# Writing out every engine loop of a two-layer mixer and expert-retrieval step

## The reference, cut to what matters

```python
def peer_ffn(h, w_q, sub_keys, u_tab, v_tab):
    q = (tok @ w_q).reshape(T, PEER_HEADS, 2, PEER_KEY_DIM // 2)
    s = jnp.einsum('thsk,snk->thsn', q, sub_keys)
    sv, si = lax.top_k(s, PEER_TOPK)                    # 16 best of 128 keys, on two sides
    cand_s = sv[..., 0, :, None] + sv[..., 1, None, :]  # 256 pairs, and again the 16 best
    cand_i = si[..., 0, :, None] * N_KEYS + si[..., 1, None, :]
    top_s, top_pos = lax.top_k(cand_s, PEER_TOPK)
    idx = jnp.take_along_axis(cand_i, top_pos, axis=-1)
    g = jax.nn.softmax(top_s, axis=-1)
    a = jax.nn.gelu(jnp.einsum('tkd,td->tk', u_tab[idx], tok))
    return jnp.einsum('tk,tkd->td', g * a, v_tab[idx])
```

## Time and profile before

| | |
|---|---|
| median of three runs | 6189.84 us |
| the three runs | 6198.78, 6189.19, 6189.84 us |
| span of the profiled execution, first to last instruction | 6172.5 us |
| median over that span | 17.3 us |
| expert stage, layer 1, first gather to the end of the last | 1083 to 3060 us |
| expert stage, layer 2 | 4143 to 6125 us |
| busy: PE, DVE, POOL, ACT | 4637.5, 2873.5, 2863.0, 450.7 us |
| mean granted TensorE clock | 0.938 |
| bytes moved by gathers | 1342.34 MB of 1489.50 MB |

### The profile page before, as it was taken

How to read it: one execution, slowest core, us unless ns; L and a number is a source line. 1 busy time by engine, 2 the same in 40 slices (tenths; PEclk the granted TensorE clock), 3 DMA queues, 4 the chain that set the end, 5 groups by cost and what they waited for, 6 DMA issues and landing times.

```text
span 6172.5 us, 45021 instructions
## 1 busy us (share of the span) xinstructions
PE 4637.5 (75%) x12847; PEld 2050.5 (33%) x12847; DVE 2873.5 (47%) x6890; ACT 450.7 (7%) x830; POOL 2863.0 (46%) x2569
## 2 busy tenths in 40 slices
PE   7999996566666766667789999956676766666666
PEld 3645544122222222222245555532222222222222
DVE  2241113665656656545312411146657566565543
ACT  1131010000000000000010400100000000000000
POOL 0000000676776767777500000017767777677774
PEclk9999998899999999999999999978999999999999
DMA  7101110899999999999851012119999999999996
GB/s 231 55 28 36 60 55 14 318 346 340 339 353 330 337 333 331 348 332 368 310 170 63 21 43 66 48 45 325 352 343 333 339 329 339 340 335 354 345 354 245
DMA packets 504201, 1489.50 MB, mean 241 GB/s; under 512 B 49632, under 2 KB 172976, under 8 KB 502578
## 3 DMA queue, kind: packets, MB, share of 16 engines
q0 software_dynamic: 368640, 1342.34, 59.6%
q1 hardware_dynamic: 126000, 140.54, 7.1%
q10 hardware_dynamic: 9346, 4.38, 0.3%
HBM read 1484.30 MB, written 2.79 MB: 241 GB/s over the span
## 4 chain that ended last, share of the span: by engine, by line
PE 39%; DMA 24%; issue 18%; DVE 9%; POOL 7%; ACT 1%; DVEq 1%; POOLq 0%; another core or an unknown queue 0%; PEldq 0%; PEld 0%; ACTq 0%; SPq 0%
DMA ring<-in_peer_v_dram,kt 16%; PE ps L468 10%; PE ps L822 10%; DMA ring<-in_peer_u_dram,kt 7%; POOL ring L1605 7%; PE ps L747 7%; DVE m_t L1506 3%; PE ps L511 2%; PE ps L754 2%; DVE ring L1517 2%; PE ps L552 1%; PE ps L699 1%; PE ps L679 1%; PE ps L627 1%; PE ps L499 1%
## 5 line engine op out<-in xcount | busy, mean ns | idle before, releaser
L822 PE MATMUL ps<-ring,m_t 128*128 128x512 f32 x5120 | 2655.2, 651 | 1270.3 <-DMA ring<-in_peer_v_dram,kt 913.1
L1605 POOL DMA_INDIRECT ring<-in_peer_u_dram,kt x1280 | 1363.8, 1065 | 2742.0 <-issue 1447.6
L1517 DVE CUSTOM_DVE_ANT_0 ring<-ring,m_t 128x1024 f32<-128x1024 f32 x1280 | 1553.7, 1225 | 1465.9 <-DMA ring<-in_peer_u_dram,kt 1403.3
L822 PEld LDWEIGHTS ps<-ring,m_t 128*128 128x128 f32 x5120 | 940.1, 201 | 2969.5 <-DMA ring<-in_peer_v_dram,kt 1797.0
L1605 POOL DMA_INDIRECT ring<-in_peer_v_dram,kt x1280 | 1498.6, 1171 | 519.1 <-issue 286.3
L468 PE MATMUL ps<-h_t,ring 128*128 128x128 f32 (+1 forms) x1536 | 426.1, 438 | 21.9 <-ACT h_t L895 14.6
L747 PE MATMUL ps<-h_t,ring 128*128 128x128 f32 (+1 forms) x1536 | 425.1, 435 | 11.7 <-issue 9.1
L1506 DVE TENSOR_SCALAR m_t<-cst,kt 128x128 f32<-128x128 f32 x1280 | 343.8, 367 | 21.5 <-issue 11.6
L468 PEld LDWEIGHTS ps<-h_t,ring 128*128 128x128 f32 x1536 | 235.1, 192 | 214.6 <-issue 209.7
L747 PEld LDWEIGHTS ps<-h_t,ring 128*128 128x128 f32 x1536 | 235.4, 191 | 199.6 <-issue 199.6
L1087 ACT ACTIVATE kt<-kt 128x16 f32<-128x16 f32 x80 | 17.3, 216 | 3439.7 <-DVEq L1533 1905.6
(11 more groups left out here) (212 smaller groups left out, 2592.1 us busy)
## 6 DMA issues: line engine op xcount, KB each, us to landing
ring<-in_w_ada_dram SPq DMA_DIRECT2D x48, 1024.0 KB, 6.7
ring<-in_w_in_dram SPq DMA_DIRECT2D x36, 1024.0 KB, 5.4
ring<-in_peer_u_dram,kt POOLq DMA_INDIRECT x1280
ring<-in_peer_v_dram,kt POOLq DMA_INDIRECT x1280
ring<-in_peer_wq_dram SPq DMA_DIRECT2D x16, 1024.0 KB, 5.5
ring<-in_tables_dram SPq DMA_DIRECT2D x10, 1024.0 KB, 4.8
ring<-in_w_out_dram SPq DMA_DIRECT2D x8, 1024.0 KB, 5.0
ring<-in_w_branch_c_dram SPq DMA_DIRECT2D x8, 512.0 KB, 6.5
```

The lines of the kernel that those rows point to most:

```text
L822: mm = pe.matmul(y_acc[:, cols], diag[h % 2][:, k, :], rows_v[:, s, cols], start=n == 0, stop=n == EXPERTS - 1)
L1517: dve.tensor_tensor_reduce(rows_u[:, s, :], rows_u[:, s, :], tok_cur, 1.0, 0.0, ALU.mult, ALU.add, dots[:, n:n + 1]).then_inc(rows_u_free. ...
L1605: pool.indirect_dma_start(rows[:, s, :], None, table, bass.IndirectOffsetOnAxis(ap=idx, axis=0)).then_inc(came[s].sem, 16)
```

## The change

All `Fori` loops on all five engines become Python loops, so that the program holds every round of every layer one behind the other, without branches, and every wait is against a constant. In `gather` the separate instruction that carried the wait goes, and the wait stands on the gather itself; the semaphore `passed_pool` goes with it. The `carry_waits` on the other engines stay. No work is moved to another engine, and the order in which an engine does its work stays.

```diff
-        passed = {"pe": sem("passed_pe"), "dve": sem("passed_dve"), "pool": sem("passed_pool"),
+        passed = {"pe": sem("passed_pe"), "dve": sem("passed_dve"),
                   "sp": sem("passed_sp")}
...
-            with sp.Fori(0, LAYERS) as l:
-                with sp.Fori(0, N_ADA // SLOTS) as i:
+            for l in range(LAYERS):
+                for i in range(N_ADA // SLOTS):
...
-            with pe.Fori(0, LAYERS) as l:
+            for l in range(LAYERS):
...
-                with pe.Fori(0, N_ADA // SLOTS) as i:
+                for i in range(N_ADA // SLOTS):
...
-                with pe.Fori(0, D // CW) as i:
+                for i in range(D // CW):
...
-                with pe.Fori(0, 2) as i:
+                for i in range(2):
...
-                with dve.Fori(0, 1) as j:
+                for j in range(1):
                     peer_tile(j, None, True)
-                with dve.Fori(0, TILES - 2) as j:
+                for j in range(TILES - 2):
                     peer_tile(j + 1, j, True)
-                with dve.Fori(TILES - 2, TILES - 1) as j:
+                for j in range(TILES - 2, TILES - 1):
                     peer_tile(j + 1, j, False)
...
                 s = n % slots
                 pool.wait_ge(free.sem, free.after(l, n + 1 - slots) + j * EXPERTS)
-                carry_waits(pool, "pool")
                 pool.indirect_dma_start(rows[:, s, :], None, table, bass.IndirectOffsetOnAxis(
                     ap=idx, axis=0)).then_inc(came[s].sem, 16)
...
-                with pool.Fori(0, TILES - 1) as j:
+                for j in range(TILES - 1):
                     pool.wait_ge(idx_ready.sem, idx_ready.after(l, 2) + j)
```

More of the change, by code:

```diff
@@ L408, in _ @@
                     load(l, CH_WIN + s, tables[s].rearrange("p (j n) -> p j n", j=STILES))
-                with sp.Fori(0, D // CW) as i:
+                for i in range(D // CW):
                     for s in range(3):
@@ L421, in _ @@
                     load(l, CH_OUT + s, cols_of(w_out, l, s * CW))
-                with sp.Fori(0, 2) as i:
+                for i in range(2):
                     for s in range(SLOTS):
@@ L831, in peer_tile @@
                     close_turn(out, mm)
-                with pe.Fori(0, TILES - 1) as j:
+                for j in range(TILES - 1):
                     peer_tile(j, "peer_out", j * 2, True)
@@ L896, in add_shift @@
                                    bias=mod[:, shift + k, 1:2], scale=amp[:, which, k, 1:2]).then_inc(h_ready.sem, 1)
-            with act.Fori(0, LAYERS) as l:
+            for l in range(LAYERS):
                 def put(dst, src):
@@ L1034, in _ @@
                         take_values(v // TILES)
-                with act.Fori(0, D // CW) as i:
+                for i in range(D // CW):
                     for n in range(6):
@@ L1049, in _ @@
                 add_shift(l, KC, 3 * KC)
-                with act.Fori(0, 2) as i:
+                for i in range(2):
                     for n in range(8):
@@ L1097, in _ @@
                 take_tokens("tok", 0, 0)
-                with act.Fori(0, TILES - 1) as j:
+                for j in range(TILES - 1):
                     peer_tile(j, True)
@@ L1149, in normalise @@
                     dve.tensor_tensor(h_t[:, k, :], x_t[:, k, :], rinv[:, :], ALU.mult).then_inc(scaled.sem, 1)
-            with dve.Fori(0, LAYERS) as l:
-                with dve.Fori(0, N_ADA // SLOTS) as i:
+            for l in range(LAYERS):
+                for i in range(N_ADA // SLOTS):
                     for n in range(SLOTS):
@@ L1328, in _ @@
                 dve.drain().then_inc(merged_credit.sem, 2)
-                with dve.Fori(0, D // CW) as i:
+                for i in range(D // CW):
                     for n in range(6):
@@ L1608, in _ @@
             u_rows, v_rows = (w.rearrange("l n d -> (l n) d") for w in (peer_u, peer_v))
-            with pool.Fori(0, LAYERS) as l:
+            for l in range(LAYERS):
                 def u_row(j, n):
@@ L1626, in later_heads @@
                         v_row(j, n)
-                with pool.Fori(0, 1) as j:
+                for j in range(1):
                     pool.wait_ge(idx_ready.sem, idx_ready.after(l, 1) + j)
@@ L1640, in _ @@
                     later_heads(j + 1)
-                with pool.Fori(TILES - 1, TILES) as j:
+                for j in range(TILES - 1, TILES):
                     for n in range(LAST + ROWS_V, EXPERTS):
```

## The result

| | before | after |
|---|---|---|
| median | 6189.51 us (4 runs) | 6125.37 us (6110.89 to 6131.81, 4 runs) |
| ratio | | 0.9897, 95% interval 0.9877 to 0.9917 |
| profiled execution: span, time | 6172.5 us, 6174.3 (estimated: span + 1.8) | 6121.4, 6123.24 us |
| before the first gather | 1083.5 us | 1083.3 us |
| expert stage, layer 1, layer 2 | 1976.2, 1981.5 us | 1961.8, 1951.8 us |

The change makes the kernel 64 us faster. The forecast was 6132 us, between 5900 and 6190, and faster with a chance of 0.81.

A forecast was written before the change was run, and what follows sets the result against it. POOL's issue of gathers set the expert stages' pace, with the DMA engines just behind and DVE holding POOL up. Gains of 25 + 8 + 15 + 10 = 58 us took 6189.8 to 6132 us, range 5900 to 6190.

The forecast's parts named there:

- The 0.30 gap: Between POOL's gathers in a row: removing instructions there leaves the gap at 0.30 us; gain nothing, at most 708 us.
- The wake: POOL's gather start after a late buffer release: up to 0.37 us less in 198 places, 73 us; a third taken, 25.
- Branches back on POOL: At six tile steps on POOL, branches cost about 2.65 us more than a gap; 8 of 16 us taken.
- The stall on DVE: DVE's stall before L1361, the first maximum of second key scores, put to the loop's branch; 15 of 17 us taken.
- PE's short loops: PE's branches in conditioning, merge and query projection cost about 0.55 us each; gain 10 us, bounds 5 and 15.
- the gap shrinks: Rival: the gap between POOL's gathers falls from 0.30 to 0.15 us, giving about 5900 us; chance 0.20.
- slower: Rival: the gather's own wait ends POOL's working ahead; 0.1 us more per gap gives 6370 us; chance 0.08.
- nothing much on the path: Rival: POOL's and DVE's savings go into buffer waits, only PE's loop gains stay, 6180 us; chance 0.10.

The follow-up runs named there:

- wait_apart: Changed kernel with the wait back on an instruction of its own ahead of each gather, no loops: 6176.0 us, 0.9954 of the kernel before.
- pool_alone: Kernel before with only POOL's part changed, its loops written out and each gather carrying its wait: 6174.1 us, 0.9941 of the kernel before.
- rest_alone: Changed kernel with POOL's hardware loops, registers and separate waiting instruction put back: 6180.8 us, 0.9969 of the kernel before.
- quarter_dots_first: Changed kernel with DVE's diagonals in four lots and each quarter's dots ahead of its selection part: 6036.2 us, 0.9729 of the kernel before.

## Why the prediction was right, and where not

**The 0.30 gap: right.** This decided the size. The gap stands at 0.30 with the wait on the gather and with six instructions more ahead of it. What I made of it was too broad, though: "what stands before a gather is done while the one before it still runs" holds for the usual gap, but six instructions cost 60 us in other places, where POOL's stream fell behind.

**The wake: right in kind, too small.** I allowed a gain of 0.37 us in each place and took a third of 198 places, 25 us. It is 0.54 us (0.81 to 0.27), and wait_apart puts the term at 33 us, of which some 22 belong to the wait's place. The wrong step is the floor: I had a wake end no sooner than a usual gap and 0.14 us for the semaphore, 0.44, but it is shorter than a gap. "A third of it" was nearly right, for a reason that I didn't have: in 62 of the 83 places where DVE freed the buffer and the gather started 0.27 us later, the next dot ran already and held the gather, which took about 1.7 us. The rule that I quoted from the Trainium skill, Perfetto Trace Analysis, section "DMA Instruction — SWDGE (GPSIMD)", that the instruction sits in a wait queue by itself until its semaphores are there, gave 101 us if all lay on the path. For one wake the trace agrees with it: all of the 0.51 us went, and 0.03 more. On the path at most a third of it came.

The Trainium skill, SBUF — State Buffer, section "SBUF: two separate sides", has a rule on the hold: a DVE operation with two inputs in SBUF and a GpSimd operation that reads SBUF share a pair of ports, and the later one is blocked for the whole of the first. The trace agrees for one order. Of 1155 gathers that start while a dot runs, 968 end 0.81 us after it, and with half as long dots the hold fell from 464 to 150 us. It doesn't show the other order: 770 dots start less than 1 us after a gather with no dot at its start, and they take the usual 1.23 us and the gathers 0.94 (medians). The gather at 1442.09 and the dot at 1442.16 are such a pair.

**Branches back on POOL: the cause right, the gain not shown.** All six stalls of 2.7 to 3.2 us are gone, also in pool_alone and wait_apart, and they are back in rest_alone. I took 8 of the 16 us as won. The v gather behind waits for PE all the longer, as foreseen, and takes up more than I allowed: 2 to 6 us stay won against the kernel before, and nothing against rest_alone (20.7 us with the branches, 20.8 without).

**The stall on DVE: wrong, in cause and in worth.** I put it to the branch because it was always at the same place of the loop's body. That doesn't tell a branch from anything else that happens once in a tile. The row said "remote", and L1361 waits for the key scores of PE, whose records had ended 3 us before. I took that record for the end, though the page itself says that the ends of matmuls are modelled. The term was 15 us; 2 came, less than one execution differs from another. That it "counts fully" is doubtful too, since quarter_dots_first is without the stall and no faster.

**PE's short loops: right.** Outside the two stages the kernel before took 2214.8 and 2218.8 us in its two profiles, the changed one 2207.9 and 2199.9: 7 to 19 us, where I took 10. All profiles together say the same: the three profiles in which PE has its loops (the third is pool_alone's, 2219.4) have 2217.7 us outside the stages in the mean; the eleven without have 2205.6, none above 2211.4. That is 12 us. Of layer 1's share a second profile shows more than the first; the clock may have a hand in it.

**The sum** was 58 us, and 61 to 64 came, partly by luck: DVE's stall gave 13 us less than its term, the branches 2 to 6 less, the wake and the instruction some 8 more, and 12 to 15 us have no term (some 2 of them outside the stages, by the means above). Of the rivals, "the gap shrinks" and "slower" fell with the gap; "nothing much on the path" fell with pool_alone.

## What to carry to other kernels

Put the wait for a buffer onto the gather itself, and keep other instructions out of POOL's stream: here that was half of the gain (33 us of 61), and all the loops together the other half (28). A stall at the same place in every round is no sign of a branch; ask first which semaphore the instruction waits for, and don't trust the recorded end of a matmul for it. When an engine frees buffers one by one, cut its other long work (here 4.3 us of diagonals) into lots between the releases: that won 116 us on top, more than the whole change.

## What was unexpected in the hardware

- A gather that carries its wait starts 0.27 us after the release, less than the 0.30 us between two gathers in a row; with the wait on an instruction ahead of it, 0.81 us.
- Six increments ahead of each gather leave the usual gap at 0.30 us and cost some 60 us all the same: 398 of the 15360 increments take over 0.5 us, where 17 ns is usual, and POOL's stream falls behind in 104 places.
- A gather that starts while a dot runs is held until 0.81 us after the dot; a dot that starts while a gather runs is not held.
- PE's key scores (16 products of 128x128, recorded as 1.95 us) were through 1.4 to 4.1 us after their recorded end in eight of eight tiles, when a drain stood behind them.
- With 2 KB pieces in place of 4 KB, and half dots in both, the DMA engines move 183 GB/s in place of 367 (2600 to 2900 us), and the two stages with their 2560 gathers take 3758 us in place of 3804.
